# A two-block transformer kernel: layer edges of the second block reordered, gating projection one column later

## The chip, the cores and the metric

One core of a Trainium2 chip runs the whole program. The metric is the device time of one execution in microseconds (us); the median of several runs counts. Engines are named as in the profile: PE (TensorE, matrix products), PEld (its weight loads), DVE (VectorE), ACT (ScalarE), POOL (GpSimd), SP (SyncE, which issues the transfers). PSUM is the memory that PE writes, SBUF the one that all engines read.

## The reference, cut to what matters

The program computes two blocks in float32 on 256 tokens of width 1024. The first (two layers with pooling, convolution, indexed attention and a convolutional feed-forward) isn't touched. The second has four layers of kinds A, B, C, A over 256 latent tokens `x` and 256 context tokens `xc`:

```python
for i in range(4):
    sh, sc, gt = split(silu(c) @ ada_w[i] + ada_b[i], 3)        # and shc, scc, gtc from c_ctx
    h  = rms_norm(x,  norm_g[i]) * (1.0 + sc)  + sh
    hc = rms_norm(xc, norm_g[i]) * (1.0 + scc) + shc
    u, z = split(h @ w_in, [n_mix_cols])                        # u: q, k, v;  z: gate
    o, oc = mixer(u, uc)                                        # A: grouped, B: neighbourhood, C: differential attention
    x = x + gt * ((o * silu(z)) @ w_out)
    if i < 3:
        xc = xc + gtc * ((oc * silu(zc)) @ w_out)
```

`rms_norm` divides by the root of the mean square over the 1024 features (plus 1e-6). In the last layer only the latent part is needed.

## The kernel before

Activations are held with features on the 128 partitions: `x2[P, 8, 512]` is x (columns 0 to 255) and xc (256 to 511) in 8 chunks. All weights pass as 512 KB tiles (128 x 8 x 128) through a ring of four slots (`ring`); SP sends tile t as soon as slot t % 4 is free, in the order of the tiles. A tile of kind R is used as it is and frees its slot when PE is through with it. A tile of kind P is split: ACT writes its high part `w_hi` (line 874), POOL the low part `w_lo` (line 294), and the slot is free after the low part. A product of a split tile is three matmuls per chunk of K, on lines 421 to 423 (high x high, high x low twice); a chunk of output is 24 matmuls of 512 columns. Results go to three PSUM banks in turn.

One layer (`block2(L)` on each engine) runs:

1. The squares of the 8 chunks of x2 (ACT, line 1076, four buffers in `sq`), each summed over the features by a matmul with a matrix of 1/1024 into the PSUM bank `st` (PE, line 668).
2. rstd: ln and exp (ACT, lines 1078, 1079), its square (1080), and a Newton step on DVE (`refine`, lines 1251, 1255, 1256). `h2 = x2 * rstd` in 8 chunks (DVE, line 1483), then scale and shift: the latent half by ACT (line 1083, semaphore `h_full`), the context half by POOL (line 1830, semaphore `h_ctx`). ACT and DVE split h2 in `h_hi` and `h_lo`.
3. Two rows of adaLN weights of a later layer (`ada_row`, 4 tiles of kind R each, matmuls of 2 columns, line 465), while PE would have nothing else.
4. Value chunks (line 688), key chunks, the first query chunk and the first gate chunk z(0).
5. Eight columns of attention, c = 0 to 7, of `NU` units each (6, in layer 3 4). In column c PE works on the scores (line 727), transposes (657) and values (759, 763) of its units, and between them on pieces of "fillers": `q(c+1)` and `z(c+1)`. In column 7 the fillers are two adaLN rows (none in layer 3).
6. The gate: `gate_out(c)` on DVE multiplies the output with `silu(z)` (line 1624); `split_gated` (lines 1634, 1635, both DVE) makes high and low parts of it, two chunks a unit in column 7.
7. The output projection: 8 chunks; the first two are interleaved with the last values. Each chunk is scaled by the gate gt into `rot` (ACT, lines 1217, 1218) and added to x2 (DVE, line 1675).

Every engine works through its own queue in the order in which the code issues it; semaphores hold it back. `hi_parts` and `split_to` put the weight splits into the queues of ACT and POOL at fixed places: ACT's stands ahead of the evacuation (`op`) of a chunk two tiles earlier, POOL's in `q_side(c)` behind the rope product `sin_mul` (line 1745) and, in column c, behind `q_pow` (line 1846).

The step 1 of the next layer is as follows before (ACT, then PE):

```python
for m in range(KC):
    act.wait_ge(S["x2_ready"], (L - 1) * KC + m + 1)
    if m >= 4:
        act.wait_ge(S["sq_summed"], L * KC + m - 3)
    act.activation(sq[:, m % 4, :], x2[:, m, :], ACT.Square).then_inc(S["x2_sq"], 1)
...
for m in range(KC):
    pe.wait_ge(S["x2_sq"], L * KC + m + 1)
    ins = pe.matmul(st[:, :], cw("ones_d"), sq[:, m % 4, :], start=(m == 0), stop=(m == KC - 1))
```

## Time and profile before

| | |
|---|---|
| median of 3 runs | 2466.03 us (2460.39 to 2472.28) |
| the profiled execution | 2468.51 us |
| its span, first to last instruction | 2466.4 us |
| PE busy | 2223.9 us (90%), mean granted clock 0.932 |
| DVE, ACT, POOL busy | 1314.5, 1033.0, 912.5 us |
| second block | about 984 us to the end |

The profile is one execution. Its views give, in us from the start of the span: the timeline (start, duration, engine, line, operation, output<-input by the program's names without their numbers, so that `x2` reads `x` and `st` reads `stat`, then in brackets the idle time before it and what ended it), windows (busy time of each engine in a stretch, and the clock that the throttle granted TensorE there, 1.00 for 2.4 GHz and 0.50 for 1.2 GHz), and the chain of waits that ended last. A float32 matmul is recorded as two.

### The profile page before, as it was taken

To read this page: it belongs to the slowest core of one execution; us is meant where nothing else is said; L and a number is where in the kernel's file an instruction comes from. 1 tells how busy PE (TensorE), PEld (TensorE's weight loads), DVE (VectorE), ACT (ScalarE), POOL (GpSimd) and SP (SyncE) were. 2 spreads that over 40 slices of the span, in tenths; PEclk is the share of its full clock that TensorE was granted. 3 is DMA by queue.
4 is the path that set the end of the run, shared out by engine and by line. 5 is a ranking of instruction groups with operands and counts; after the bars stand their busy time and mean duration, and the time that the engine had idled before them with its cause. 6 is when DMAs were issued, how large, how long until landed. Compare 5 with 4: busy or idle time off the path is not lost.

```text
span 2466.4 us, 39608 instructions
## 1 busy us (share of the span) xinstructions
PE 2223.9 (90%) x14736; PEld 1854.9 (75%) x14736; DVE 1314.5 (53%) x2688; ACT 1033.0 (42%) x1978; POOL 912.5 (37%) x588
## 2 busy tenths in 40 slices
PE   6969899998788998899999898999889899888898
PEld 5868899987788998667766876776778566666677
DVE  4594556547844664356651235556224766723565
ACT  4433466453435654533322244332334445425332
POOL 0444378005453840333422133332313434333443
PEclk8989999989899999899979999999989899888898
DMA  6423556653345655311122321112232111223121
GB/s 220 146 85 107 187 174 193 188 171 113 103 128 172 196 189 188 120 35 44 41 88 68 120 86 56 61 52 73 86 106 92 52 43 35 79 76 120 52 69 52
DMA packets 72848, 262.92 MB, mean 107 GB/s; under 512 B 8032, under 2 KB 10208, under 8 KB 72416
## 3 DMA queue, kind: packets, MB, share of 16 engines
q1 hardware_dynamic: 71392, 256.31, 32.5%
q0 software_dynamic: 1280, 4.20, 0.6%
q8 instruction: 118, 1.93, 0.3%
q14 instruction: 58, 0.48, 0.1%
HBM read 259.43 MB, written 1.05 MB: 106 GB/s over the span
## 4 chain that ended last, share of the span: by engine, by line
PE 65%; DVE 18%; issue 6%; ACT 6%; POOL 5%; DMA 0%; DVEq 0%; ACTq 0%; SPq 0%; POOLq 0%
PE gemm L421 13%; PE gemm L422 12%; PE gemm L423 12%; PE gemm L688 6%; PE score L727 5%; DVE r L1348 3%; PE obank L759 3%; PE tbank L657 3%; DVE d L1294 2%; PE stat L668 1%; PE obank L763 1%; POOL arena L1830 1%; POOL w_lo L294 1%; DVE zt L1256 1%; DVE small L1554 1%
## 5 line engine op out<-in xcount | busy, mean ns | idle before, releaser
L294 POOL TENSOR_TENSOR w_lo<-ring,w_hi 128x1024 fp32r<-128x1024 f32 x252 | 605.6, 2408 | 556.0 <-ACT w_hi L874 554.7
L421 PE MATMUL gemm<-g_hi,w_hi 128*128 128x256 f32 x1344 | 395.2, 294 | 42.3 <-POOL w_lo L294 28.1
L421 PE MATMUL gemm<-h_hi,w_hi 128*128 128x512 f32 (+1 forms) x928 | 388.5, 419 | 12.4 <-DVE h_lo L1635 9.6
L874 ACT ACTIVATE w_hi<-ring 128x1024 fp32r<-128x1024 f32 x344 | 361.7, 1053 | 81.3 <-PE gemm L423 39.9
L422 PE MATMUL gemm<-g_lo,w_hi 128*128 128x256 f32 x1344 | 383.9, 286 | 0.0
L423 PE MATMUL gemm<-g_hi,w_lo 128*128 128x256 f32 x1344 | 383.8, 286 | 0.0
L422 PE MATMUL gemm<-h_lo,w_hi 128*128 128x512 f32 (+1 forms) x928 | 353.1, 381 | 0.0
L423 PE MATMUL gemm<-h_hi,w_lo 128*128 128x512 f32 (+1 forms) x928 | 352.8, 380 | 0.0
L421 PEld LDWEIGHTS gemm<-g_hi,w_hi 128*128 128x128 f32 x1344 | 264.7, 197 | 62.2 <-POOL w_lo L294 36.2
L1189 ACT ACTIVATE pr<-score,small 128x512 f32<-128x512 f32 (+1 forms) x192 | 128.0, 669 | 392.8 <-DVE small L1556 390.5
L421 PEld LDWEIGHTS gemm<-h_hi,w_hi 128*128 128x128 f32 x928 | 180.5, 195 | 148.4 <-issue 108.2
L422 PEld LDWEIGHTS gemm<-g_lo,w_hi 128*128 128x128 f32 x1344 | 265.3, 197 | 0.2
L423 PEld LDWEIGHTS gemm<-g_hi,w_lo 128*128 128x128 f32 x1344 | 264.8, 197 | 0.0
L423 PEld LDWEIGHTS gemm<-h_hi,w_lo 128*128 128x128 f32 x928 | 180.7, 195 | 35.1
L422 PEld LDWEIGHTS gemm<-h_lo,w_hi 128*128 128x128 f32 x928 | 181.6, 196 | 27.3 <-issue 3.8
L727 PE MATMUL score<-arena,d 64*128 64x512 f32 x256 | 153.9, 683 | 32.6 <-DVE d L1294 30.6
L1554 DVE TENSOR_REDUCE small<-score 128x1 f32<-128x512 f32 (+1 forms) x144 | 99.5, 691 | 139.1 <-PE score L727 67.5
L688 PE MATMUL gemm<-ring,arena 128*128 128x128 f32 x1280 | 153.5, 285 | 12.7 <-POOL arena L1830 11.7
L688 PEld LDWEIGHTS gemm<-ring,arena 128*128 128x128 f32 x1280 | 152.3, 201 | 14.8 <-issue 14.8
L294 DVE TENSOR_TENSOR w_lo<-ring,w_hi 128x1024 fp32r<-128x1024 f32 x92 | 114.7, 1251 | 77.8 <-ACT w_hi L874 77.3
L1745 POOL TENSOR_TENSOR rot<-shf,cst 128x512 f32<-128x512 f32 (+1 forms) x36 | 46.1, 1281 | 272.1 <-DVE shf L1287 272.1
L759 PEld LDWEIGHTS obank<-arena,pt 128*128 128x128 f32 x896 | 124.6, 207 | 9.5 <-issue 2.6
(278 smaller groups left out, 3885.4 us busy)
## 6 DMA issues: line engine op xcount, KB each, us to landing
ring<-wall SPq DMA_DIRECT2D x478, 512.0 KB, 3.7
r<-nbias POOLq DMA_DIRECT2D x16, 256.0 KB, 3.0
cst<-consts SPq DMA_DIRECT2D x1, 2340.5 KB, 10.3
r<-x_t SPq DMA_DIRECT2D x1, 1024.0 KB, 4.7
x<-ctx_t SPq DMA_DIRECT2D x1, 1024.0 KB, 15.5
y_t<-x SPq DMA_DIRECT2D x4, 256.0 KB, 2.3
d<-pos SPq DMA_DIRECT2D x1, 128.0 KB, 10.2
```

The source lines that it names most:

```text
L294: eng.tensor_tensor(w_lo[:, q % SPLITS, :, :], ring[:, t % RING, :, :], w_hi[:, q % SPLITS, :, :].bitcast(F), ALU.subtract)\
L421: pe.matmul(out, w[0][:, k, :], x[0], start=start, stop=False)
L422: pe.matmul(out, w[0][:, k, :], x[1], start=False, stop=False)
L423: return pe.matmul(out, w[1][:, k, :], x[0], start=False, stop=stop)
L657: ins = pe.transpose(tb[:, j * P:(j + 1) * P], src(j), ident)
L688: ins = pe.matmul(out[:, t * P:(t + 1) * P], h2[:, k, t * P:(t + 1) * P], w[:, k, :], start=(k == 0), stop=(k == KC - 1))
L727: ins = pe.matmul(bk[:, :], q[:, t * P:(t + 1) * P], kT[a:a + HD, kc, :], start=True, stop=True)
L759: ins = pe.matmul(ob[:, 0:W], pb[:, j * P:(j + 1) * P], vv[:, j, col:col + W], start=(j == 0), stop=(j == 3))
L874: act.activation(w_hi[:, q % SPLITS, :, :], ring[:, t % RING, :, :], ACT.Copy).then_inc(S["hi_ready"], 1)
L1189: ins = act.activation(dst[:, a:z], src[:, a:z], ACT.Exp, scale=rq, bias=NBm[:, 2 * i4 + q:2 * i4 + q + 1], accum_out=SUM[:, 2 * i4 + q:2 ...
L1348: ins = dve.scalar_tensor_tensor(cacc[:, j, :], win, w, cacc[:, j, :], ALU.mult, ALU.add)
L1554: seq(dve.tensor_reduce(MX[:, i2:i2 + w], bk[:, :] if t < 2 else bk[:, :].rearrange("p (a n) -> p a n", a=2), AX, ALU.max))
```

## The change

It has these parts, all in the second block:

- The gate chunk z(c) (c > 0) is a filler of column c, not c - 1. Column 0 has q(1) and then one adaLN row (4 tiles) as fillers, column 7 has z(7) and then the other row; in layer 3 column 0 has q(1) alone and column 7 z(7) alone. The tiles of q(2), and of the first two chunks of the output projection, are placed ahead of the rows' tiles and fetched by their number (`early`). ACT's evacuation of z and POOL's `z_side` follow one column later.
- The high part of the gated output is made by ACT (`gated_high`), the low part by DVE; both in the second half of column 7, seven chunks over its units.
- For layers 1 to 3, seven of the eight squares and of their sums move from the edge into the output projection of the layer before: on ACT the square of chunk m - 1 stands behind the evacuation of chunk m, on PE its sum behind chunk m. The table load of ACT moves ahead of the projection.
- rstd is refined in the PSUM bank `st`: the addition of eps is done while ACT computes the exp, two DVE instructions follow, and line 1483 multiplies by `st`.
- The first value chunk waits for the latent chunks of h one by one, and for the context half only ahead of its third quarter.

```diff
-        put("qz", L, "PP" * KC)
-        put("last", L, "RRRR" * FILL_SLOT[L])
-        put("w_out", L, "P" * KC)
+        row = "RRRR" if FILL_SLOT[L] else ""
+        put("qz", L, "PPPP" + row + "P" * 12)
+        put("w_out", L, "PP" + row + "P" * 6)
...
+            def square_sum(L, m):
+
+                pe.wait_ge(S["x2_sq"], L * KC + m + 1)
+                pe.matmul(st[:, :], cw("ones_d"), sq[:, m % 4, :], start=(m == 0), stop=(m == KC - 1)).then_inc(S["sq_summed"], 1)
...
-                for m in range(KC):
-                    pe.wait_ge(S["x2_sq"], L * KC + m + 1)
-                    ins = pe.matmul(st[:, :], cw("ones_d"), sq[:, m % 4, :], start=(m == 0), stop=(m == KC - 1))
-                    ins.then_inc(S["sq_summed"], 1)
+                if L == 0:
+                    for m in range(KC):
+                        square_sum(L, m)
+                else:
+                    square_sum(L, KC - 1)
...
-                pe.wait_ge(S["h_full"], (6 + L) * KC)
-                pe.wait_ge(S["h_ctx"], (1 + L) * KC)
                 for j in range(nk):
                     w, out = tile(), bank()
                     for t in range(4):
+                        if j == 0 and t == 2:
+                            pe.wait_ge(S["h_ctx"], (1 + L) * KC)
                         for k in range(KC):
+                            if j == 0 and t == 0:
+                                pe.wait_ge(S["h_full"], (5 + L) * KC + k + 1)
...
                         if c + 1 < KC:
+                            yield from chunk(h(NQ), NQ, None, early if c == 1 else None)
+                        if c == 1 and slot:
+                            ada_columns()
+                        if c:
                             yield from chunk(h(NQ), NQ)
-                            yield from chunk(h(NQ), NQ)
-                        else:
-                            for _ in range(FILL_SLOT[L]):
-                                yield from ada_row()
+                        if c in (0, KC - 1) and slot:
+                            early = n["tile"]
+                            yield from row_tiles(1 if c == 0 else 2)
...
                 for m in range(2, KC):
                     run(chunk(h(NQ), NQ))
+                    if need_ctx:
+                        if m == 2:
+                            square_sum(L + 1, 0)
+                        square_sum(L + 1, m - 1)
...
+                def gated_high(c):
+
+                    act.wait_ge(S["gated_ready"], L * KC + c + 1)
+                    act.activation(h_hi[:, c, 0:NQ], gated[:, place(c, nk), 0:NQ], ACT.Copy).then_inc(S["gated_hi"], 1)
...
-                        if c == KC - 1 and FILL_SLOT[L] and u in ((NU // 2, NU - 1) if FILL_SLOT[L] == 2 else (NU - 1,)):
-                            ada_row_out()
+                        if u == NU // 2 and c == KC - 1:
+                            evac_z(c)
+                        if c == KC - 1:
+                            for i in splits_at(NU, u):
+                                gated_high(i)
+                        if c in (0, KC - 1) and u == NU - 1 and slot:
...
                     act.sem_inc(S["yo_evac"], 1)
+                    if need_ctx and m:
+                        stream_square(L + 1, m - 1)
...
+                dve.wait_ge(S["var_read"], 5 + L + 1)
+                seq(dve.tensor_scalar(st[:, :], st[:, :], EPS, None, ALU.add))
                 dve.wait_ge(S["rstd_ready"], 5 + L + 1)
-                refine(rstd[:, :], zh[:, 0, :], st[:, :], 1.0, EPS)
+                seq(dve.scalar_tensor_tensor(st[:, :], zh[:, 0, :], -0.5, st[:, :], ALU.mult, ALU.mult))
+                seq(dve.scalar_tensor_tensor(st[:, :], st[:, :], 1.5, rstd[:, :], ALU.add, ALU.mult))
```

How this moves instructions shows in each engine's order. ACT, output projection of layer 0, chunks 2 and 3 (874, in the change 919, is a weight's high part; 1217 and 1218, now 1291 and 1292, evacuate a chunk), before:

```order
L874 ACTIVATE w_hi<-ring 128x1024 [waits act_step,split_done,wslot2]
L1217 ACTIVATE rot<-gemm,ada 128x256 [waits x2_ready,split_done]
L1218 ACTIVATE rot<-gemm,ada 128x256
L874 ACTIVATE w_hi<-ring 128x1024 [waits act_step,split_done,wslot3]
L1217 ACTIVATE rot<-gemm,ada 128x256 [waits x2_ready,split_done]
L1218 ACTIVATE rot<-gemm,ada 128x256
L874 ACTIVATE w_hi<-ring 128x1024 [waits act_step,split_done,wslot0]
L1217 ACTIVATE rot<-gemm,ada 128x256 [waits x2_ready,split_done]
L1218 ACTIVATE rot<-gemm,ada 128x256
```

and with the change (1114 is a square):

```order
L1114 ACTIVATE sq<-x 128x512 [waits act_step,x2_ready]
L919 ACTIVATE w_hi<-ring 128x1024 [waits split_done,wslot1]
L919 ACTIVATE w_hi<-ring 128x1024 [waits split_done,wslot2]
L1291 ACTIVATE rot<-gemm,ada 128x256 [waits x2_ready,split_done]
L1292 ACTIVATE rot<-gemm,ada 128x256
L1114 ACTIVATE sq<-x 128x512 [waits act_step,x2_ready]
L919 ACTIVATE w_hi<-ring 128x1024 [waits split_done,wslot3]
L1291 ACTIVATE rot<-gemm,ada 128x256 [waits x2_ready,split_done]
L1292 ACTIVATE rot<-gemm,ada 128x256
L1114 ACTIVATE sq<-x 128x512 [waits act_step,x2_ready]
L919 ACTIVATE w_hi<-ring 128x1024 [waits split_done,wslot0]
```

Each evacuation is now followed by the square of the chunk before it, and that by the weight split that stood there.

PE, end of the projection of layer 0 (the last product of chunk 7, then the sums on line 668, then the adaLN rows), before:

```order
L422 MATMUL gemm<-h_lo,w_hi 128x512
L423 MATMUL gemm<-h_hi,w_lo 128x512
L668 MATMUL stat<-sq,cst 128x512 [waits x2_sq] x8
L465 MATMUL gemm<-ring,sc_c 2x128 [waits wslot2,bank_read]
L465 MATMUL gemm<-ring,sc_c 2x128 x7
```

and with the change, the end of chunk 2 of the same projection (675 is a sum, 432 to 434 the products):

```order
L433 MATMUL gemm<-h_lo,w_hi 128x512
L434 MATMUL gemm<-h_hi,w_lo 128x512
L675 MATMUL stat<-sq,cst 128x512 [waits x2_sq] x2
L432 MATMUL gemm<-h_hi,w_hi 128x512 [waits bank_read,slot_used1]
L433 MATMUL gemm<-h_lo,w_hi 128x512
```

All eight sums stood behind the last chunk; now two stand behind chunk 2 and one behind each of chunks 3 to 6, ahead of the next chunk, and two behind chunk 7.

POOL, from the key chunks of layer 0 to the middle of column 1 (1745, now 1818: rope product; 294: low part of a weight; 1846, now 1923: power for q; 1853 and 1854, now 1930 and 1931: z_side), before:

```order
L1745 TENSOR_TENSOR rot<-shf,cst 128x512 [waits roped,shuffled] x2
L294 TENSOR_TENSOR w_lo<-ring,w_hi 128x1024 [waits hi_ready]
L1846 TENSOR_TENSOR small<-small 128x8 [waits qss_read]
L294 TENSOR_TENSOR w_lo<-ring,w_hi 128x1024 [waits hi_ready]
L1853 TENSOR_TENSOR zs<-zt,zh 128x512 [waits z_evac]
L1854 TENSOR_TENSOR zs<-zs,zh 128x512 [waits pool_step]
L1745 TENSOR_TENSOR rot<-shf,cst 128x512 [waits roped,shuffled]
L294 TENSOR_TENSOR w_lo<-ring,w_hi 128x1024 [waits hi_ready]
L1846 TENSOR_TENSOR small<-small 128x8 [waits qss_read]
```

and with the change:

```order
L1818 TENSOR_TENSOR rot<-shf,cst 128x512 [waits roped,shuffled] x2
L1923 TENSOR_TENSOR small<-small 128x8 [waits qss_read]
L294 TENSOR_TENSOR w_lo<-ring,w_hi 128x1024 [waits hi_ready]
L1930 TENSOR_TENSOR zs<-zt,zh 128x512 [waits z_evac]
L1931 TENSOR_TENSOR zs<-zs,zh 128x512 [waits pool_step]
L1818 TENSOR_TENSOR rot<-shf,cst 128x512 [waits roped,shuffled]
L294 TENSOR_TENSOR w_lo<-ring,w_hi 128x1024 [waits hi_ready]
L1923 TENSOR_TENSOR small<-small 128x8 [waits qss_read]
```

The low part of q(1) stood ahead of the power instruction and now stands behind it; the next one, behind the rope product of q(1), was that of q(2)'s tile and is so still, but an adaLN tile of column 0 now follows it in the same ring slot.

## Rows read from the trace of the kernel before

**Rows 1.** Page, chain that ended last: shares of the span by engine.
```profile
PE 65%; DVE 18%; issue 6%; ACT 6%; POOL 5%; DMA 0%; DVEq 0%; ACTq 0%; SPq 0%; POOLq 0%
```

**Rows 2.** Timeline of ACT, layer 0 projection and edge: start us, us, operation, idle.
```profile
1326.13 0.47 ACT L1217 ACTIVATE rot<-gemm,ada 128x256 f32<-128x256 f32 x1 [3.45 <-PE gemm L423]
...
1327.22 1.06 ACT L874 ACTIVATE w_hi<-ring 128x1024 fp32r<-128x1024 f32 x1 [0.25 <-ACT rot L1218]
1331.73 0.47 ACT L1217 ACTIVATE rot<-gemm,ada 128x256 f32<-128x256 f32 x1 [3.45 <-PE gemm L423]
...
1352.56 0.63 ACT L1076 ACTIVATE sq<-x 128x512 f32<-128x512 f32 x1 [0.42 <-PE stat L668]
```

**Rows 3.** Timeline of PE, edge from layer 0 to 1.
```profile
1345.92 9.98 PE L668 MATMUL stat<-sq,cst 128*128 128x512 f32 x16 [3.02 <-ACT sq L1076]
1355.83 1.93 PE L465 MATMUL gemm<-ring,sc_c 128*2 128x128 f32 x64
...
1364.30 1.03 PE L465 MATMUL gemm<-ring,sc_c 128*2 128x128 f32 x16 [0.23 <-DMA ring<-wall]
1368.74 6.44 PE L688 MATMUL gemm<-ring,arena 128*128 128x128 f32 x41 [3.41 <-POOL arena L1830]
```

**Rows 4.** Timeline of PE, edges from layer 1 to 2 and 2 to 3.
```profile
1787.58 8.83 PE L668 MATMUL stat<-sq,cst 128*128 128x512 f32 x16 [3.03 <-ACT sq L1076]
...
2223.59 7.13 PE L668 MATMUL stat<-sq,cst 128*128 128x512 f32 x16 [3.02 <-ACT sq L1076]
```

**Rows 5.** Timeline of DVE, edge from layer 0 to 1.
```profile
1343.92 0.69 DVE L1675 TENSOR_TENSOR x<-x,rot 128x512 f32<-128x512 f32 x1 [4.91 <-ACTq L1220]
...
1360.24 5.30 DVE L1483 TENSOR_TENSOR arena<-x,rstd 128x512 f32<-128x512 f32 x8
```

**Rows 6.** Windows, layer 2: length, busy PE, PEld, DVE, ACT, POOL; PEclk, DMA share, GB/s.
```profile
1993.40:1996.80 3.40, 1.64 (x6) 0.81 (x6) 1.70 (x2) 2.74 (x6) 2.70 (x3) 1.00 0.34 66
1996.80:2000.20 3.40, 3.40 (x13) 2.85 (x11) 3.05 (x8) 0.87 (x2) 2.36 (x2) 0.50 0.22 88
...
2078.70:2082.10 3.40, 3.40 (x17) 2.26 (x16) 1.71 (x5) 1.62 (x4) 3.40 (x2) 1.00 0.54 154
```

**Rows 7.** First column of layer 0: DVE, POOL, PE, then the ring transfers.
```profile
1053.44 2.82 DVE L1294 TENSOR_TENSOR d<-d,rot 128x512 f32<-128x512 f32 x1 [0.98 <-POOL rot L1745]
...
1053.37 2.34 POOL L294 TENSOR_TENSOR w_lo<-ring,w_hi 128x1024 fp32r<-128x1024 f32 x1
1056.41 1.67 POOL L1846 TENSOR_TENSOR small<-small 128x8 f32<-128x8 f32 x1 [0.71 <-DVE small L1530]
...
1079.90 1.43 POOL L1745 TENSOR_TENSOR rot<-shf,cst 128x512 f32<-128x512 f32 x1 [16.91 <-DVE shf L1287]
1081.30 2.39 POOL L294 TENSOR_TENSOR w_lo<-ring,w_hi 128x1024 fp32r<-128x1024 f32 x1
...
1077.40 1.00 PE L763 MATMUL obank<-arena,pt 128*128 128x64 f32 x8
...
1084.38 1.09 PE L727 MATMUL score<-arena,d 64*128 64x512 f32 x2 [0.50 <-DVE d L1294]
...
DMA to landing us min/median/max: 3.2/3.7/13.0
```

**Rows 8.** Windows over the last columns of layers 0 (two stretches), 1, 2, 3.
```profile
1252.90:1266.30 13.40, 11.28 (x109) 7.13 (x109) 10.87 (x27) 3.00 (x8) 4.15 (x3) 1.00 0.45 156
1266.30:1291.60 25.30, 25.06 (x133) 16.00 (x133) 11.03 (x27) 8.45 (x23) 5.13 (x3) 0.50 0.31 102
1700.70:1734.30 33.60, 27.91 (x241) 18.62 (x241) 23.89 (x57) 11.22 (x30) 9.22 (x6) 0.89 0.45 138
2130.50:2166.40 35.90, 26.06 (x204) 16.97 (x205) 26.48 (x57) 16.55 (x49) 11.21 (x10) 0.73 0.45 144
2414.80:2433.90 19.10, 15.95 (x71) 11.41 (x71) 15.35 (x37) 4.94 (x11) 6.75 (x5) 0.73 0.17 56
```

**Rows 9.** Timeline of ACT, last column of layer 1.
```profile
1720.54 0.72 ACT L1183 ACTIVATE pr<-scratch,small 128x512 f32<-128x512 f32 x1 [5.11 <-DVE small L1551]
```

More of the change, by code:

```diff
@@ L312, in turn_step, with place, splits_at @@
             return 4 if kind == "C" else 2
+        def place(c, nk):
+            return (c + nk) % KC
+        def splits_at(NU, u):
+            upto = lambda v: max(0, -(-(KC - 1) * (v - NU // 2 + 1) // (NU - NU // 2)))
+            return range(upto(u - 1), upto(u))
         def closes(kind, u):
@@ L349, in ada_rows @@
         def ada_rows(r):
-            return (pr[:, 1:3, :] if r < sum(FILL) else shf)[0:2, r % 2, :]
+            if r < sum(FILL):
+                return pr[0:2, 1 + r % 2, :]
+            return shf[0:2, r % 2, :] if (r - sum(FILL)) % 4 < 2 else rstd[0:2, :]
         def nrm(m):
@@ L806, in block2 @@
                 last = [(KC - 1, u) for u in range(NU) if closes(kind, us[u])]
-                for _ in range(FILL_SLOT[L]):
+                if slot:
                     ada_columns()
@@ L810, in block2 @@
                 values(*last[-2])
-                w, out = [tile(), tile(1)], [bank(), bank()]
+                if not slot:
+                    early = n["tile"]
+                    n["tile"] += 2
+                w, out = [split_tile(early), split_tile(early + 1)], [bank(), bank()]
                 def w_out_part(m):
@@ L847, in seq, with op @@
                 act.wait_ge(S["act_step"], n["step"])
-            def op(tiles=1, at=None):
+            def op(tiles=1, at=None, ahead=AHEAD):
                 n["tile"] += tiles
@@ L855, in op @@
                 elif tiles:
-                    hi_parts(n["tile"] - 1 + AHEAD)
+                    hi_parts(n["tile"] - 1 + ahead)
                     t = n["tile"] - 1
@@ L1200, in block2 @@
                         if u == NU // 2 and c + 1 < KC:
-                            evac_q(c + 1)
-                        if c == KC - 1 and FILL_SLOT[L] and u in ((NU // 2, NU - 1) if FILL_SLOT[L] == 2 else (NU - 1,)):
-                            ada_row_out()
-                for _ in range(FILL_SLOT[L]):
+                            evac_q(c + 1, early if c == 1 else None)
+                            if c == 1 and slot:
+                                ada_columns_out()
+                        if u == NU // 2 and c == KC - 1:
[4 more added lines that the diff above has]
+                        if c in (0, KC - 1) and u == NU - 1 and slot:
+                            early = n["tile"]
+                            n["tile"] += 1 if c == 0 else 2
+                            ada_row_out(AHEAD if c == 0 else 1)
+                if slot:
                     ada_columns_out()
+                else:
+                    early = n["tile"]
+                    n["tile"] += 2
                 if kind == "C":
@@ L1661, in block2 @@
                         if c == KC - 1:
[L1662 to L1664 removed]
+                            for i in splits_at(NU, u):
+                                split_gated(i)
                 last = [(KC - 1, u) for u in range(NU) if closes(kind, us[u])]
@@ L1870, in block2 @@
                 split_to(AT["w_out", L] + 1)
+                z_side(KC - 1)
                 if kind == "C":
```

111 lines of the change are left out of this document (69 added, 42 removed).

## The prediction

> **What bounds the kernel now.** The chain of waits [rows 1] is 65% TensorE (PE), so an edit is worth what it adds to or takes from PE's queue. I then read the four places that the change touches, in the second block (layers 0 to 3, kinds A, B, C, A; an edge is the way from one layer's output projection to the next layer's first value chunk).
>
> - The output projection is PE's alone: chunks end every 5.60 us, and ScalarE (ACT) takes each up within 0.03 us of its end [rows 2].
> - At the first edge PE idles 3.02 us, spends 9.98 us on the eight sums of squares, has the two adaLN rows done 9.5 us later (1355.83 to 1365.33), idles 3.41 us and starts the value chunk at 1368.74 [rows 3]. That last idle ends with GpSimd (POOL), which writes the context half of h. From the end of the chunk before: 25.8 us. At the two other edges idle and sums take 3.03 + 8.83 and 3.02 + 7.13 us [rows 4].
> - The last column of each layer has adaLN rows for filler, or nothing. In layer 0 it begins with 13.4 us at the full clock; then TensorE's granted clock is 0.50 (1.2 GHz) for 25.3 us. Layers 1, 2, 3 take 33.6, 35.9 and 19.1 us at 0.89, 0.73, 0.73 [rows 8].
>
> **The change, part by part.**
>
> *Squares inside the projection.* ACT's new queue is: evacuate chunk m, then square x of chunk m-1. PE's is: chunk m, then the sum of square m-1, then chunk m+1. The input of the square has been there for 4 us, but the square stands behind an evacuation that can't begin until chunk m ends. So PE always waits at the sum. The next ACT instruction starts 1.09 us after the evacuation's start (1326.13 to 1327.22, where a weight split stands now), and a square takes 0.63 us [rows 2]: PE waits 0.03 + 1.09 + 0.63 + 0.05 = 1.8 us. The sum is 7.13 / 8 = 0.89 us [rows 4]. Each of m = 2 to 6 thus delays the projection by 2.7 us (at m = 2 two sums, the first inside the wait): 13.5 us an edge, **+40.5** for three. Behind the waiting sum stands all of PE's queue, no other engine is late by it: weight split m+3 moves 0.7 us back and has over 5 us of slack. Bounds: 0.9 us a step, if the square were somehow ready (+13), and 3.6, if the sum also runs at half clock (+54); the rows of this very place give 2.7.
>
> *What the waits do to the clock.* Once a column of layer 2 PE idles 1.7 us. A stretch with such an idle (PE busy 1.64 of 3.40 us) was followed by one at clock 0.50; the stretch after another was at 1.00; of five such idles four cost the clock and one didn't [rows 6]. Half clock over 3.4 us costs 1.7 us. There are four waits of 1.8 us inside each projection, 12 in all, at arbitrary places; I take half of them: **+10**, from 0 (none) to +20 (all). The Trainium skill (TensorE: Matmul & The Clock Gate, A second HAM failure mode) says that short idles between groups of matmuls make the clock swing and that what is lost is the way back up between the bursts; by that rule every wait would pay, which is the +20 end. The trace shows both outcomes, so I stay between.
>
> *What the edge saves.* After the last chunk only two sums remain. The seventh starts 1.8 us after the chunk; the eighth square needs the last addition, which starts 1.0 us after the chunk and takes 0.69 [rows 5], so it follows at once: both done at 3.6 us, against 13.0, 11.9 and 10.2 now: **-24.3**. From there to the value chunk it is now 12.8 us. The changed refinement has one VectorE (DVE) instruction fewer after rstd (about 0.7 us, like the addition of [rows 5]), the product starts 3.6 instead of 4.3 us after the sums [rows 3, 5], and with 8 x 0.66 us and one ACT pass of some 0.6, as the square takes, the latent half is there at 9.5. The adaLN rows also end at 9.5, since their weight tiles arrive no faster. The value chunk now waits for latent chunks one by one and for the context only in its third quarter, so it starts at 9.5: -3.3 at each of four layer starts, **-13.2**. Bounds -2 to -21 (nothing but the refinement; or the clock comes back earlier too, 2 us each). The table load leaves the edge for a place behind PE's last products; its cover is chunk 2, 5.6 us long. A product read from PSUM I put at 0: bounds -1 and +1.
>
> Edges together: 40.5 + 10 - 24.3 - 13.2 = **+13.0**.
>
> *First columns.* The second half loses the z chunk (5.6 us) for four tiles of an adaLN row (about 0.5 us each, 1.93 for four [rows 3]). The fourth tile takes the ring slot of q(2), and that is freed by POOL's low part, which in the queue stands behind the rope product of q(1). In layer 0: values of unit 2 end at 1078.40, rope product at 1079.90, low part 1081.30 to 1083.69 and then a transfer of at least 3.2 us [rows 7]: the tile lands 8.5 us or more after those values, I take 8.8. PE has 3.1 us of work until it needs it, so it waits 5.7; then 1.5 us end the column. That is 10.3 us after the values against 5.98 now (1084.38) [rows 7], less 2.4 for lighter filler before: +1.9, and 2.1 for a clock that falls in such a wait: +4 in layers 0 and 2. In layer 1, without rope, 2.4 us of waiting and a first q chunk that is late (below): +3. Layer 3 has no rows, only a lighter column: -1. **+10**, from -9 (no wait decides) to +18. The low part of q(1) now follows a 1.67 us power instruction instead of standing ahead of it, so the first filler waits 2.1 us for it. In A and C this comes back: the rope end of q(0) took 2.82 us while a low part ran on POOL, where without one it is the 0.69 of such an operation [rows 5, 7]. The Trainium skill (SBUF — State Buffer, Who interferes with whom) has the rule: a DVE operation with two SBUF inputs and a GpSimd operation that reads SBUF exclude each other for a whole instruction. Here the trace agrees; without it, the sum would be 2 us more in three layers.
>
> *Last columns.* The z chunk fills their first half at the usual density. In the second half, DVE and ACT hand the gated splits to each other: maximum (1 us), exp (0.72) [rows 9], then high parts by ACT, then low parts by DVE, and only then the next unit's maximum: about 4 us a unit, with the weight split (1.06) and z evacuation ahead in unit 3 some 7. ACT's adaLN row comes after it all. 14 us for the first half + 15 for the second + 3 for row and columns + 2 to 3 of port clashes: 34.5. Against 38.7, 33.6, 35.9: -4, +1, -1; layer 3: 0. **-4**, from -20 (PE's pace) to +8. Gate to last split: ACT's hop adds 0.2 us x 4, **+1**.
>
> Sum: 13.0 + 10 - 4 + 1 = **+20**. The profiled execution took 2468.5 us (span 2466.4), 2.5 above the median of the runs; so 2488.5 on its scale, **2486** on the median's.
>
> **Rivals.**
> (A) No measurable change (0.5% either way is about what a measurement of this kernel can tell from none): waits as forecast, but the clock never falls in the projection (-10) and the last columns come down to about 32 us (-10 in place of -4): 13 - 10 + 10 - 10 + 1 = +4, 2470 us. For it: one idle of five was free [rows 6].
> (B) Faster, by one mechanism, the clock: z chunks keep PE fed, the last columns run at the full clock and PE's pace (layer 0: 13.4 + 25.3 / 2 + 5.6 - 1.9 = 29.7 us; -9, -4, -6, -1), no wait drops it in the projection (-10), the value chunks find it up (-8), and in the first columns only the tile's own wait stays (+5): 13 - 10 - 8 - 20 + 5 + 1 = -19, 2447 us. It decides where a unit of the last column stays under some 4 us. For it: 25.3 us at 0.50 are there to be won [rows 8]. Against it: the handover, and that the waits of the projection stay in any case.
> (C) Much slower: between waits the clock comes back late, so that a chunk of 5.6 us averages 8.4: 15 x 2.8 = 42 in place of 10: +52, 2518 us. Against it: every drop in [rows 6] lasted one stretch.
> (D) That the squares leave the edge and cost nothing is what the title says; it needs square m-1 ahead of evacuation m in ACT's queue, and the order of instructions has it behind.
>
> **Numbers.** Forecast 62%, A 20%, B 11%, C 7%. Range: the forecast's own 2470 to 2506 (columns and clock at their bounds one at a time); to leave out no more than 2 in 10 it reaches down over A to 2456 and up to 2510. Slower by over 0.5%: forecast and C, less a tail: 0.68; within: 0.21; faster: 0.11.
>
> **What would show it.** Right: six waits of PE at the stat sums for each edge, the later five of some 1.8 us, named after ACT's square; projections about 13 us longer; from the last chunk to the value chunk about 13 us; waits on the ring in the first columns; less half clock in the last columns, but DVE waiting for h_hi. Wrong: sums that follow their chunk without idle, last columns under 30 us, or no DMA wait in the first columns.

## The result, and the profile after

The changed kernel takes 2515.48 us (median of 4 runs, 2508.42 to 2520.96) against 2463.21 us before: a ratio of 1.0205, 95% interval 1.0165 to 1.0245. That is 52 us slower by the medians. I had forecast 20 us slower, with a range that ended at 2510: the sign was right, the size was not.

The profiled execution took 2517.51 us, its span is 2515.4 us (before 2468.51 and 2466.4), so the two traces differ by 49.0 us. Cut at the same places of the second block, they differ as follows (first scores, first and last products and first value products of each layer, from the timeline of PE; us, after less before):

| stretch | layer 0 | 1 | 2 | 3 | sum |
|---|---|---|---|---|---|
| value chunk to first score | -4.0 | -0.4 | -2.3 | -2.6 | -9.3 |
| column 0 | +6.4 | +1.5 | +4.2 | +1.3 | +13.4 |
| column 1 | +2.7 | +3.3 | +2.2 | +4.9 | +13.1 |
| columns 2 to 6 | +0.6 | 0 | +0.6 | +1.5 | +2.7 |
| column 7 to first product of the projection | -2.7 | +3.7 | +5.0 | +1.7 | +7.7 |
| projection | +14.6 | +16.9 | +12.3 | +5.1 | +48.9 |
| last product to the next value chunk | -10.5 | -8.2 | -8.2 | 0 | -26.9 |

The table adds up to 49.6; the second block begins 0.5 us earlier in the later trace.

The waits of PE show the same. What PE waited for, with us in total, times and the longest, before (L421 is the first product of a split tile, L465 an adaLN row, L688 a value chunk, L668 a sum of squares):

```profile
PE gemm L421 <- POOL w_lo L294: 30.9, 26, 4.0
...
PE gemm L465 <- DMA ring<-wall: 21.7, 20, 2.8
PE gemm L688 <- POOL arena L1830: 11.7, 4, 3.4
...
PE stat L668 <- ACT sq L1076: 11.4, 4, 3.0
```

and after (L476 is an adaLN row, L432 the first product of a split tile, L675 a sum of squares, L708 a value chunk):

```profile
PE gemm L476 <- DMA ring<-wall: 44.9, 24, 7.3
PE gemm L432 <- POOL w_lo L294: 40.1, 28, 4.7
PE stat L675 <- ACT sq L1114: 30.6, 19, 1.8
...
PE gemm L708 <- DMA ring<-wall: 3.7, 4, 2.1
```

The wait for the context half of h is gone from the list (11.7 us), and three others have grown by 23, 9 and 19 us. The page's chain of waits, of which [rows 1] is the line before, has DMA in it now (0% before):

```profile
PE 66%; DVE 16%; ACT 7%; issue 5%; POOL 4%; DMA 2%; ACTq 0%; DVEq 0%; SPq 0%; POOLq 0%
```

**The projection of layer 0**, timeline of PE, which answers to [rows 3]:

```profile
1327.70 1.13 PE L675 MATMUL stat<-sq,cst 128*128 128x512 f32 x2 [1.75 <-ACT sq L1114]
1328.26 0.80 PE L432 MATMUL gemm<-h_hi,w_hi 128*128 128x512 f32 x1
...
1336.18 1.13 PE L675 MATMUL stat<-sq,cst 128*128 128x512 f32 x2 [1.75 <-ACT sq L1114]
...
1361.76 1.98 PE L675 MATMUL stat<-sq,cst 128*128 128x512 f32 x4 [1.81 <-ACT sq L1114]
1363.68 1.93 PE L476 MATMUL gemm<-ring,sc_c 128*2 128x128 f32 x64
...
1375.29 1.01 PE L708 MATMUL gemm<-ring,arena 128*128 128x128 f32 x3 [2.11 <-DMA ring<-wall]
```

and of ACT in the same place, which answers to [rows 2]:

```profile
1325.99 0.47 ACT L1291 ACTIVATE rot<-gemm,ada 128x256 f32<-128x256 f32 x1 [5.87 <-PE gemm L434]
1326.37 0.47 ACT L1292 ACTIVATE rot<-gemm,ada 128x256 f32<-128x256 f32 x1
1327.02 0.63 ACT L1114 ACTIVATE sq<-x 128x512 f32<-128x512 f32 x1 [0.19 <-ACT rot L1292]
1327.56 1.04 ACT L919 ACTIVATE w_hi<-ring 128x1024 fp32r<-128x1024 f32 x1
```

The square starts 1.03 us after the evacuation's start and PE has waited 1.75 us for it: the picture of the forecast. The sums, and so the chunks, come every 8.5 us (1327.70 to 1336.18) instead of every 5.60.

**The clock.** Windows from the sums behind chunk 2 to the last product, for layers 0, 1, 2, then over the last columns of layers 0 to 3, which answer to [rows 8] (length, busy time of PE, PEld, DVE, ACT and POOL, granted clock, DMA):

```profile
1317.30:1360.00 42.70, 34.66 (x133) 24.24 (x131) 3.46 (x5) 10.18 (x19) 10.45 (x8) 1.00 0.25 85
1771.70:1816.00 44.30, 36.29 (x133) 25.14 (x131) 3.46 (x5) 10.19 (x18) 8.48 (x4) 0.96 0.21 60
2223.20:2265.80 42.60, 34.60 (x133) 24.20 (x131) 4.10 (x5) 10.18 (x18) 9.15 (x4) 1.00 0.22 62
```

```profile
1258.10:1294.10 36.00, 28.45 (x197) 21.02 (x197) 21.73 (x47) 13.98 (x33) 14.48 (x8) 0.84 0.33 107
1711.50:1748.90 37.40, 28.53 (x199) 21.04 (x197) 23.72 (x50) 14.26 (x34) 14.48 (x8) 0.83 0.26 87
2158.40:2199.40 41.00, 25.46 (x161) 17.37 (x161) 24.42 (x50) 19.53 (x51) 14.04 (x12) 0.77 0.27 90
2456.90:2477.80 20.90, 15.81 (x96) 12.21 (x95) 14.18 (x33) 7.78 (x21) 8.77 (x7) 0.90 0.25 76
```

Behind the first sums of each projection the clock stays at 2.4 GHz but for one stretch of layer 1, although PE stands still for 1.8 of every 8.5 us.

**Column 0 of layer 0.** POOL, then PE, which answer to [rows 7]:

```profile
1075.87 1.44 POOL L1818 TENSOR_TENSOR rot<-shf,cst 128x512 f32<-128x512 f32 x1 [17.36 <-DVE shf L1363]
1077.27 2.34 POOL L294 TENSOR_TENSOR w_lo<-ring,w_hi 128x1024 fp32r<-128x1024 f32 x1
```

```profile
1083.45 1.03 PE L476 MATMUL gemm<-ring,sc_c 128*2 128x128 f32 x16 [6.03 <-DMA ring<-wall]
```

The low part of q(2) ends at 1079.61 (1077.27 and 2.34), PE gets the tile that goes into its slot 3.8 us later, and has then stood still for 6.03 us. In layers 1 and 2 the same wait is 3.10 and 7.28 us.

**The last column of layer 1.** PE, then ACT, DVE and POOL around PE's long idle:

```profile
1738.61 1.09 PE L668 MATMUL tbank<-cst,pr 128*128 128x128 f32 x4 [5.52 <-ACT pr L1242]
```

```profile
1728.68 1.04 ACT L919 ACTIVATE w_hi<-ring 128x1024 fp32r<-128x1024 f32 x1
1729.63 0.58 ACT L1187 ACTIVATE zt<-gemm 128x512 f32<-128x512 f32 x1
1730.11 0.58 ACT L1188 ACTIVATE zh<-gemm 128x512 f32<-128x512 f32 x1
1730.87 1.67 ACT L1195 ACTIVATE h_hi<-arena 128x512 fp32r<-128x512 f32 x3 [0.18 <-ACT zh L1188]
1737.70 0.72 ACT L1242 ACTIVATE pr<-scratch,small 128x512 f32<-128x512 f32 x1 [5.16 <-DVE small L1630]
```

```profile
1731.61 4.45 DVE L1709 TENSOR_TENSOR h_lo<-arena,h_hi 128x512 fp32r<-128x512 f32 x3 [2.69 <-ACT h_hi L1195]
1735.98 0.47 DVE L1626 SCALAR_TENSOR_TENSOR scratch<-score,small,r 128x256 f32<-128x256 f32 x1
...
1743.26 1.29 DVE L1709 TENSOR_TENSOR h_lo<-arena,h_hi 128x512 fp32r<-128x512 f32 x2 [0.38 <-ACT h_hi L1195]
```

```profile
1732.12 1.72 POOL L1930 TENSOR_TENSOR zs<-zt,zh 128x512 f32<-128x512 f32 x1
1733.92 1.59 POOL L1931 TENSOR_TENSOR zs<-zs,zh 128x512 f32<-128x512 f32 x1
```

DVE waits 2.69 us for the first high half, then makes three low halves (L1709) in 4.45 us, and only then scales the next unit's scores, takes their maximum and lets ACT do the exp (L1242): ACT has been idle for 5.16 us, PE for 5.52.

**The projection of layer 3**, PE and ACT:

```profile
2492.55 0.58 PE L432 MATMUL gemm<-h_hi,w_hi 128*128 128x256 f32 x1 [4.73 <-POOL w_lo L294]
```

```profile
2488.29 0.47 ACT L1292 ACTIVATE rot<-gemm,ada 128x256 f32<-128x256 f32 x1 [0.25 <-ACT rot L1292]
2489.01 2.95 ACT L919 ACTIVATE w_hi<-ring 128x1024 fp32r<-128x1024 f32 x3 [0.24 <-ACT rot L1292]
```

Three high parts of weight tiles stand together behind the evacuation of chunk 1. POOL can make its low part of chunk 2's tile only after the first of them, and PE waits 4.73 us for it. I had not spoken of this place at all.

### The profile page after: what moved, and what is told of

It reads as the page before. It is cut to its first block, busy times and chain, and to the rows that moved or that the text cites. A ratio compares the mean times of both kernels' runs of the same rounds, so it can differ in the third digit from the quotient of the medians.

```text
span 2515.4 us, 39615 instructions
## 1 busy us (share of the span) xinstructions
PE 2227.4 (89%) x14736; PEld 1858.9 (74%) x14736; DVE 1293.3 (51%) x2656; ACT 1047.2 (42%) x2009; POOL 899.5 (36%) x588
## 4 chain that ended last, share of the span: by engine, by line
PE 66%; DVE 16%; ACT 7%; issue 5%; POOL 4%; DMA 2%; ACTq 0%; DVEq 0%; SPq 0%; POOLq 0%
PE gemm L432 14%; PE gemm L433 12%; PE gemm L434 12%; PE gemm L708 6%; PE score L747 5%; DVE r L1424 3%; PE obank L779 3%; PE tbank L668 3%; DMA ring<-wall 2%; POOL w_lo L294 2%; PE stat L675 1%; DVE d L1370 1%; PE obank L783 1%; ACT w_hi L919 1%; DVE h_lo L1709 1%
## 5 line engine op out<-in xcount | busy, mean ns | idle before, releaser
L432 PE MATMUL gemm<-g_hi,w_hi 128*128 128x256 f32 x1344 | 398.2, 296 | 38.8 <-POOL w_lo L294 26.2
L432 PE MATMUL gemm<-h_hi,w_hi 128*128 128x512 f32 (+1 forms) x928 | 398.8, 430 | 22.4 <-POOL w_lo L294 13.9
L432 PEld LDWEIGHTS gemm<-g_hi,w_hi 128*128 128x128 f32 x1344 | 265.8, 198 | 58.9 <-POOL w_lo L294 34.0
L432 PEld LDWEIGHTS gemm<-h_hi,w_hi 128*128 128x128 f32 x928 | 183.8, 198 | 163.0 <-issue 106.7
L708 PE MATMUL gemm<-ring,arena 128*128 128x128 f32 x1280 | 152.7, 284 | 4.6 <-DMA ring<-wall 3.7
L708 PEld LDWEIGHTS gemm<-ring,arena 128*128 128x128 f32 x1280 | 151.2, 200 | 6.8 <-DMA ring<-wall 5.7
## 6 DMA issues: line engine op xcount, KB each, us to landing
cst<-consts SPq DMA_DIRECT2D x1, 2340.5 KB, 10.1
x<-ctx_t SPq DMA_DIRECT2D x1, 1024.0 KB, 15.3
```

The costliest lines, as they stand in the source:

```text
L432: pe.matmul(out, w[0][:, k, :], x[0], start=start, stop=False)
L708: ins = pe.matmul(out[:, t * P:(t + 1) * P], h2[:, k, t * P:(t + 1) * P], w[:, k, :], start=(k == 0), stop=(k == KC - 1))
```

## The experiments

Twelve kernels ran. Each is the changed kernel or the kernel before with the edit shown; every median is set against that of the kernel before in the same set of runs (2464.1, 2462.1 and 2462.8 us).

### What each of the three parts costs

**squares_at_edge**: PE's and ACT's part of the streaming undone.

```diff
-                    if need_ctx:
-                        if m == 2:
-                            square_sum(L + 1, 0)
-                        square_sum(L + 1, m - 1)
...
-                    if need_ctx and m:
-                        stream_square(L + 1, m - 1)
...
+                act.preload_act_table_set("natural_log_exp_and_others")
+                for m in range(KC):
+                    stream_square(L, m)
```

> The changed kernel with the squares and sums back at the layer's edge (ACT's table load too); columns, fillers, refinement and value waits as changed. Theory 'three parts add up' (from the two traces: the projections of the three streaming layers grew by 14.6, 16.9 and 12.3 us, of the 27 us saved behind the last chunk about 23 are the sums and their idle time): the streamed squares cost 21 us net, so 2515 - 21 = 2494 us, still 30 slower than before, with the projections of layers 0 to 2 back at 50 to 54 us from first product to last and no wait of PE in them. Rival 'the squares are the whole loss': 2465 us, level with before. Rival 'the squares are neutral, their waits only take over time that the edge gave back': 2513 to 2517 us.

Measured: 2496.31 us (ratio 1.0134, 1.0117 to 1.015). The streamed squares cost 19.2 us on the changed kernel. The projections of layers 0 to 2 are back at 51.6, 50.8 and 52.2 us. So the squares are neither the whole loss nor neutral, and the larger part, 32 us above before, lies elsewhere.

**old_columns**: the streaming, the refinement and the value waits of the change put into the kernel before; tiles, fillers, z and gated splits as before.

```diff
+                    if need_ctx:
+                        if m == 2:
+                            square_sum(L + 1, 0)
+                        square_sum(L + 1, m - 1)
...
-                refine(rstd[:, :], zh[:, 0, :], st[:, :], 1.0, EPS)
+                seq(dve.scalar_tensor_tensor(st[:, :], zh[:, 0, :], -0.5, st[:, :], ALU.mult, ALU.mult))
+                seq(dve.scalar_tensor_tensor(st[:, :], st[:, :], 1.5, rstd[:, :], ALU.add, ALU.mult))
...
-                pe.wait_ge(S["h_ctx"], (1 + L) * KC)
...
+                        if j == 0 and t == 2:
+                            pe.wait_ge(S["h_ctx"], (1 + L) * KC)
```

> The kernel before with the streamed squares, the refinement in PSUM and the value waits of the change, but with the old order of z, fillers, adaLN rows and gated splits. Theory 'three parts add up': the columns cost what the seven stretches from the first score to the first product of the projection show, +7, +8, +12 and +9 us, with the projection of layer 3 (+5), less what the shorter way from the value chunk to the first score gives back in layers 0, 2, 3 (some 9): 32 us, so 2483 us. Rival 'the columns only pay for a clock that the waits of the projection pulled down': the columns would stay long, 2505 us or more. Rival 'the squares are the whole loss': 2515 us.

Measured: 2472.51 us (1.0041, 1.0028 to 1.0055). The new columns cost 43.0 us, not the 32 expected. Two things were left out of the sum of the stretches. The last column of layer 0, 38.7 us in the trace before, takes 34.1 us here, so 4.6 us of the new column's cost had been hidden. And the ways from the last product to the next value chunk are longer with the new columns: by 1.4, 0.9 and 2.1 us between the traces of refine_waits_only (the next run) and squares_at_edge.

**refine_waits_only**: of the three hunks of old_columns, the last two alone.

> The kernel before with the refinement in PSUM and the value chunk's waits alone. Forecast term 'rest of the layer starts' said -13.2 us for four starts, so 2450 us; after the traces (value chunk to first score 4.0, 0.4, 2.3, 2.6 us shorter, of which the lighter POOL queue of the changed columns has its part) I expect -4 to -10, 2455 us. Rival: the value chunk starts earlier but then stands at its third quarter for POOL's context half, so that nothing is gained: 2463 us.

Measured: 2454.02 us (0.9961, 0.9947 to 0.9976), 10.1 us faster. The three parts can now be taken in either order: -10.1, then squares +18.5 (2472.5 less 2454.0), then columns +43.0; or columns +42.3 (2496.3 less 2454.0), then squares +19.2. That both ways give +51.4 is arithmetic. What the runs show is that the squares cost the same with the old columns as with the new ones, and so do the columns with and without the squares.

### The squares: whose order makes PE wait

**square_ahead**:

```diff
                 for m in range(KC):
+                    if need_ctx and m:
+                        stream_square(L + 1, m - 1)
                     b = op(0, early + m) if m < 2 else op()
...
                     act.sem_inc(S["yo_evac"], 1)
-                    if need_ctx and m:
-                        stream_square(L + 1, m - 1)
```

> The changed kernel with one thing else: ACT's square of chunk m-1 stands ahead of the evacuation of chunk m instead of behind it. Theory 'PE waits for a ready square behind an evacuation': the 15 waits of 1.75 to 1.81 us go, a chunk with its sum takes 5.6 + 0.9 instead of 8.5 us, 15 x 1.9 = 28 us less and up to 1 us at each end: 2486 us. Rival 'the wait moves on': the weight split behind the square is later and PE waits for the next chunk's low part instead: 2510 us or more. Rival 'dense matmuls need the waits for nothing': the sums alone cost more than 0.9 us each and the gain is under 15 us.

Measured: 2486.95 us (1.01, 1.0084 to 1.0117), 28.5 us less than the changed kernel. ACT in the projection of layer 0, where the square now waits for its input and nothing else, and what PE's sums of that projection waited for:

```profile
1324.06 0.63 ACT L1114 ACTIVATE sq<-x 128x512 f32<-128x512 f32 x1 [0.88 <-DVE x L1748]
1324.59 1.04 ACT L919 ACTIVATE w_hi<-ring 128x1024 fp32r<-128x1024 f32 x1
1328.81 0.47 ACT L1293 ACTIVATE rot<-gemm,ada 128x256 f32<-128x256 f32 x1 [3.17 <-PE gemm L434]
```

```profile
  ACT sq L1114: 1.6, 1
```

The only wait left (1.6 us, once) is that of the last sum, whose addition is really late. The weight split behind the square is done 3 us before the next evacuation: no wait moved to it. The three projections are 29.4 us shorter together (layer 0 to 2: 9.2, 11.0 and 9.2); of that the value chunks give 3.5 us back, since PE now waits 7.2 us for their tiles instead of 3.7.

**sum_later**: ACT left alone, PE asks one chunk later.

```diff
                     if need_ctx:
-                        if m == 2:
-                            square_sum(L + 1, 0)
-                        square_sum(L + 1, m - 1)
+                        square_sum(L + 1, m - 2)
+                        if m == KC - 1:
+                            square_sum(L + 1, m - 1)
```

> The changed kernel; ACT's order is left alone, and PE's sum of square m-2 (instead of m-1) stands behind chunk m, sums 5, 6 and 7 behind chunk 7. Theory 'PE waits because it asks for a square one chunk too early': the 12 waits inside the projections go as in square_ahead, 2486 us (2482 to 2490). Rival 'ACT's extra work is what delays PE, in whatever order PE asks': 2510 us or more.

Measured: 2481.47 us (1.0067, 1.0043 to 1.009; 8 runs from 2465.65 to 2490.05). The same gain as square_ahead within the scatter, without touching ACT. No cost to PE of ACT's extra work can be seen in that; what cost was that PE asked for a square which ACT's queue held behind something that PE had only just finished.

### The columns: three places

**low_part_early**:

```diff
                 for c in range(KC):
-                    split_to(qz_tile(2 * c + 2))
+                    split_to(qz_tile(2 * c + 2 + (c == 0)))
```

> The changed kernel; the one thing else is that POOL makes the low part of q(2) right behind that of q(1), ahead of z_side(0), the bias loads, the rope product and the power instruction. Theory 'the fourth adaLN tile of column 0 waits for that ring slot': the PE waits on the ring of 6.03, 3.10 and 7.28 us (layers 0, 1, 2) go, and with them the half clock that carries on into column 1 (some 2 to 4 us in each): 16 + 9 = 25, so 2490 us, columns 1 of layers 0 and 1 back near 28.2 and 27.6 us. Rival 'the transfer itself is late, whatever frees the slot': the waits stay, 2515 us. Rival 'only the idle time goes, column 1 is longer by its own work': 2499 us.

Measured: 2485.80 us (1.0094, 1.0065 to 1.0122), 29.7 us less for moving one instruction in POOL's queue. POOL makes two low parts in a row, done 17 us before the rope product:

```profile
1047.69 4.66 POOL L294 TENSOR_TENSOR w_lo<-ring,w_hi 128x1024 fp32r<-128x1024 f32 x2
...
1069.23 1.44 POOL L1818 TENSOR_TENSOR rot<-shf,cst 128x512 f32<-128x512 f32 x1 [14.28 <-DVE shf L1363]
```

The waits on the ring in column 0 are gone (one of 4.92 us stays in the last column of layer 2). Columns 0 of layers 0, 1 and 2 fell by 8.1, 3.6 and 7.3 us, columns 1 by 2.3, 2.9 and 2.4 us, and those of layer 3, which has no adaLN row, by nothing. The start of column 1 of layer 0, in the changed kernel and then here:

```profile
1086.30:1091.60 5.30, 5.30 (x13) 3.23 (x13) 2.11 (x6) 3.16 (x8) 3.99 (x2) 0.53 0.34 134
```

```profile
1072.40:1077.60 5.20, 5.20 (x23) 3.27 (x24) 2.46 (x8) 3.48 (x8) 3.99 (x2) 1.00 0.47 161
```

In 5.3 us PE got through 13 matmuls at a clock of 0.53, here through 23 at 1.00. So column 1 of this layer was long by the clock that the wait of column 0 had left behind, not by its own work.

**dve_makes_both**:

```diff
-                        if c == KC - 1:
-                            for i in splits_at(NU, u):
-                                gated_high(i)
...
-                    dve.wait_ge(S["gated_hi"], L * KC + c + 1)
+                    dve.wait_ge(S["z_evac"], (L + 1) * KC)
+                    seq(dve.tensor_copy(h_hi[:, c, 0:NQ], gated[:, place(c, nk), 0:NQ]))
```

> The changed kernel with the gated high parts made by DVE again (it waits once for the last z to be evacuated, since h_hi is read until then). Theory 'the last columns are long because ACT and DVE hand each other the high and low parts, and maximum and exp stand behind them': 2 to 4 us less in each of the last columns, 4 x 3 = 12, 2503 us. Rival 'they are long because all splits stand in three units of the second half, whoever makes them': DVE then has 0.7 us more per split, 7 a layer, and the last columns grow or stay: 2512 to 2522 us.

Measured: 2513.47 us (1.0206, 1.0173 to 1.0239). The last columns grew by 1.0, 1.0, 0.8 and 1.2 us. The first theory falls: taking the handover away, at the price of a copy on DVE for each split, gains nothing. What the handover alone costs, without that copy, no run separates.

**low_halves_later**:

```diff
                         if c == KC - 1:
-                            for i in splits_at(NU, u):
+                            for i in splits_at(NU, u - 1):
                                 split_gated(i)
+                for i in splits_at(NU, NU - 1):
+                    split_gated(i)
```

> The changed kernel; in column 7 DVE makes the low halves of a unit's share of the gated splits one unit later, behind the next unit's maximum, exp's input, instead of ahead of it. Theory 'PE's one long idle of the last column (5.52 us in layer 1) is the next unit's maximum standing behind three low halves of 1.5 us each': 3 to 5 us less in each last column, some 14 in all, 2501 us. Rival 'ACT is the jam (weight split, two passes of z, three high halves, 3.9 us ahead of the next exp), or the low halves are only moved to the column's end, where the projection's first product waits for them': 2511 to 2516 us.

Measured: 2500.14 us (1.0146, 1.0129 to 1.0163), 15.3 us less. The last columns fell by 3.5, 4.2, 6.3 and 4.9 us. DVE and PE in that of layer 1:

```profile
1730.51 0.69 DVE L1630 TENSOR_REDUCE small<-scratch 128x1 f32<-128x512 f32 x1
...
1732.54 3.56 DVE L1709 TENSOR_TENSOR h_lo<-arena,h_hi 128x512 fp32r<-128x512 f32 x3
```

```profile
1733.17 0.66 PE L668 MATMUL tbank<-cst,pr 128*128 128x128 f32 x4 [0.21 <-ACT pr L1242]
```

The maximum stands ahead of the low halves, and PE's idle of 5.52 us is 0.21; an adaLN tile then keeps it for 2.06 us (1735.89), so that the column gains 4.2.

**last_layer_splits**:

```diff
                     early = n["tile"]
                     n["tile"] += 2
+                    hi_parts(early + 2)
...
                 for m in range(KC):
+                    if m < 2 and not slot:
+                        hi_parts(early + m + AHEAD)
                     b = op(0, early + m) if m < 2 else op()
```

> The changed kernel; in layer 3 ACT makes the high parts of the weight tiles of projection chunks 2, 3 and 4 ahead of the evacuations of chunks 0 and 1, as in the kernel before, instead of behind them. Theory 'layer 3's projection waits 4.7 us for a weight split that nobody made in time': its projection falls from 33.7 to 29 us, 2510 us. Rival 'it is the ring: the tiles are not there': no change.

Measured: 2505.83 us (1.018, 1.015 to 1.021). Layer 3's projection takes 27.9 instead of 33.7 us, and PE's waits at its first products are now 1.6 and 1.2 us:

```profile
  DVE h_lo L1712: 1.6, 1
  POOL w_lo L294: 1.2, 1
```

The medians differ by 9.7 us, more than the 5.8 of the place. The rest isn't in the stretches that the edit touches, and I take it for scatter: in nine traces of kernels that are the same up to there (the changed one and all made from it but squares_at_edge) the second block's first value chunk begins anywhere from 997.6 to 1010.0 us.

### Putting them together

**three_repairs** is the changed kernel with the edits of square_ahead, low_part_early and last_layer_splits; **four_repairs** has that of low_halves_later as well.

> The changed kernel with three repairs together: square ahead of the evacuation (-28.5 alone), low part of q(2) behind that of q(1) (-29.7 alone), high parts of layer 3's projection in time (-5.8 by its projection, -9.7 by the medians). Theory 'the costs lie in different places and add up': 2515.5 - 28.5 - 29.7 - 6 = 2451 us, 11 below the kernel before. Rival 'they share one cause, a low clock': 2460 us or more.

> The three repairs with the low halves one unit later as well. By the theory of low_halves_later 14 us less than three_repairs: 2437 us, below the version with the old columns (2441.7), so that z one column later would pay after all. Rival: 2447 to 2452 us, and the old columns stay the best version.

Measured: 2453.35 us (0.9956, 0.9942 to 0.9971) and 2438.80 us (0.9897, 0.9879 to 0.9915). Each place gave together about what it gave alone: 2451 was expected of three, and the fourth gave 14.6 us against 15.3. **best_old_columns_ahead** goes the other way: the kernel before with refinement, value waits and streamed squares (old_columns), and the square ahead:

```diff
                 for m in range(KC):
+                    if need_ctx and m:
+                        stream_square(L + 1, m - 1)
                     b = op()
```

> The kernel before with the streamed squares, the refinement and the value waits, and with the square of chunk m-1 ahead of the evacuation of chunk m. Theory 'three parts add up': refine_waits_only measured 2454.0, the streamed squares cost 18.5 more on it (old_columns 2472.5), and placing the square ahead gave 28.5 on the changed kernel: 2454.0 + 18.5 - 28.5 = 2444 us, below both kernels. Rival 'the sums cost the same wherever they stand, and the edge's idle time was the cover of the adaLN tiles': 2454 us, level with refine_waits_only.

Measured: 2441.65 us (0.9922, 0.9892 to 0.9952; 2436.86 to 2456.45). Expected were 2444. four_repairs and this one beat the kernel before, by 24 and 20 us, and can't be told from each other. So z one column later, once repaired, is worth about nothing over the old columns: what it brings is not more than a few us.

## Why the forecast had the sign but not the size

Measured against forecast, part by part:

- **Squares inside the projection (+40.5): right.** Waits of 1.75 to 1.81 us against 1.8, a step of 8.5 less 5.60 = 2.9 us against 2.7. The three projections are longer by 14.3, 16.3 and 14.3 us than in squares_at_edge, 44.9 in all. square_ahead and sum_later show the mechanism from both sides.
- **What the waits do to the clock (+10): wrong.** The clock fell behind one of the twelve inner waits; the windows show 1.00, 0.96 and 1.00, so it cost about 2 us. The failed step is "There are four waits of 1.8 us inside each projection, 12 in all, at arbitrary places; I take half of them", taken from idles in the columns of layer 2 [rows 6]. By the Trainium skill (TensorE: Matmul & The Clock Gate, A second HAM failure mode) short idles between groups of matmuls make the clock swing. The trace of these projections doesn't agree: the clock stayed at 1.00 behind 11 of 12 such idles.
- **What the edge saves (-24.3 and -13.2): a little less.** From the last product to the last sum it is 3.8, 5.1 (there the clock falls to half) and 3.8 us (forecast 3.6), 12.7 against 35.1, so -22.4. The start of the layer, forecast at -13.2 for four, gave 10.1 alone, and less in the changed kernel: from the last sum to the value chunk it is 11.5, 11.4 and 11.0 us, not 9.5. The step that was mis-sized is "The adaLN rows also end at 9.5, since their weight tiles arrive no faster". In layer 0 they end 9.4 us after the sums, but then PE waits 2.11 us for the value chunk's own weight tile, which is sent behind theirs; in layers 1 and 2 the rows themselves end 10.6 and 10.5 us after the sums, and 0.82 and 0.49 us of waiting for that tile follow. The stall on POOL had covered that, and I had not asked what was late next.
- Streaming in all: forecast 40.5 + 10 - 24.3 = +26, measured +18.5 and +19.2.
- **First columns (+10): mechanism right in layers 0 to 2, price too low.** The wait for q(2)'s ring slot is 6.03 us against 5.7 forecast, 3.10 against 2.4 in layer 1, and 7.28 in layer 2. Between refine_waits_only and squares_at_edge, value chunk to column 2 is longer by 8.2, 2.0, 6.1 and 4.4 us (forecast 4, 3, 4 and -1), 20.7 in all: 7.0 gained ahead of the first score, 27.7 lost in columns 0 and 1. low_part_early took 26.6 from columns 0 and 1 of layers 0 to 2. One failed step is "and 2.1 for a clock that falls in such a wait": in layer 0 PE came back at 1083.45 and ran at half clock until 1091.3, into column 1, some 4 us lost by the half. The other is "Layer 3 has no rows, only a lighter column: -1". It was +4.4, but in good part by the clock of these traces: the same instructions of layer 3's columns 0 and 1 took 45.0 us in squares_at_edge and in the changed kernel, and 40.3 in dve_makes_both and 40.4 in square_ahead (38.7 with the old columns and their order). In the trace after, the light column 0 begins with an idle of 4.01 us and has two more of 1.35 and 2.34; PE runs at half clock for most of it and on into column 1:

```profile
2324.10:2341.40 17.30, 13.67 (x46) 8.98 (x46) 4.42 (x11) 5.61 (x12) 4.75 (x4) 0.60 0.10 30
2341.40:2354.30 12.90, 12.80 (x44) 9.64 (x44) 4.87 (x14) 1.74 (x4) 6.39 (x4) 0.50 0.24 82
```

- **Last columns (-4, and +1 for the hop): wrong sign.** Against refine_waits_only they are 2.0, 3.7, 5.0 and 1.7 us longer, +12.4. The forecast's 34.5 us were 36.0, 37.3 and 41.0. "14 us for the first half" was right: 13.6, 13.6 and 13.1 us from the column's first scores to those of its fourth unit. The failed step is "15 for the second + 3 for row and columns + 2 to 3 of port clashes", 20.5 us, which took 22.4, 23.7 and 27.9. The order was in the forecast ("then low parts by DVE, and only then the next unit's maximum"), and its price wasn't: low_halves_later puts the maximum ahead of the low halves, leaves the handover, and takes 18.9 us off the last columns, more than the 12.4 that the change had added, while dve_makes_both removes the handover and gains nothing. The baseline was off as well: in layer 0 the 34.5 us were set against 38.7, but refine_waits_only, old_columns and best_old_columns_ahead, with the same column, took 34.0, 34.1 and 34.1. The execution that gave the 38.7 was 5.3 us above the median of the kernel before. A credit of 4 us was, as far as these traces go, the clock of that one run.
- **Layer 3's projection (nothing forecast, +5.7 measured): missed.** The change fetches the first two tiles by number, and the calls that did so no longer bring the high parts of later tiles with them.

In sum the forecast was +26 for the squares, -13 for the layer starts and +7 for the columns; measured are +19, -10 and +42 to +43. The columns are some 35 us too cheap in the forecast: the first ones by 11, the last ones by 15, the projection of layer 3 by 6, and the edges behind them by 4. The other two terms were 4 us too dear together. Of the rivals, C stood at 2518 us and so near the median, but its mechanism, a clock that stays low in the projections, is not there; the time was right for a wrong reason. A had the clock of the projections right, and its last columns of 32 us wrong. B's premise, last columns at full clock, isn't there: they run at 0.84, 0.83, 0.77 and 0.90, against 0.84, 0.89, 0.72 and 0.72 in refine_waits_only. D falls by the 15 waits.

## What to carry to other kernels

When work is moved into another engine's queue, look at what stands directly ahead of the producer and at what the consumer has just finished: if the producer stands behind an evacuation of the consumer's newest result, the consumer waits every time, however early the input was ready. One place earlier for the producer or one later for the consumer gave the same 28 to 34 us. When tiles share ring slots, the price of a changed tile order is set by the engine that frees the slot, and by what stands ahead of that instruction in its queue; after a stall, count also the half clock that outlives it, and use as a baseline a length that more than one execution shows.

## What was not expected of the hardware

- Idles of 1.8 us between runs of dense matmuls (PE busy 34.66 of 42.70 us) left the clock at 1.00, while one idle of 6.03 us was followed by about 8 us at half clock, and a thin column with idles of 4.01, 1.35 and 2.34 us by 12.90 us at 0.50. The length of an idle alone doesn't tell what it costs.
- A low half of 128x512 took DVE 1.48 us (4.45 / 3) while POOL worked on z, and 0.65 us (1.29 / 2) without. By the Trainium skill (SBUF — State Buffer, Who interferes with whom) a DVE instruction with two SBUF inputs contends with a GpSimd instruction that reads SBUF. This trace agrees: POOL was busy with z for 3.31 of the 4.45 us.
- The clock over a stretch of the same instructions differs between traces of kernels that differ only elsewhere: over the last column of layer 0 it is 0.67 before and 0.84 in refine_waits_only, 38.7 and 34.0 us; over that of layer 1 0.71 in best_old_columns_ahead and 0.89 before, 38.1 and 33.7 us.
